# S5 stage: 28 dense tiles beside twelve batches (3, 2, 2) instead of ten, and three gating tiles beside each of the last four

## The reference, cut to what matters

```python
proj = h @ w_in                                  # 1024 -> 2 * 2048
u, z = jnp.split(proj, [D_INNER], axis=-1)
# per group of 16 channels (128 groups), 64 complex states:
lam_bar = jnp.exp(lam * dt)
bu = einsum('blgi,gpi->blgp', u32, b_bar)        # complex
_, states = lax.associative_scan(combine, (a, bu), axis=1)
y = einsum(real(states), c_re) - einsum(imag(states), c_im) + d_skip * u32
y = gelu(y)
y = y * sigmoid(y @ w_glu + b_glu)
y = y * silu(z)
return y @ w_out
```

## Time and profile before

| | us |
|---|---|
| median of 3 runs | 1660.5 (1659.75 to 1662.72) |
| the profiled execution | 1658.89 |
| its span, first to last instruction | 1657.1 |
| TensorE busy | 1611.1 (97%) |
| VectorE busy | 991.1 (60%) |
| ScalarE busy | 725.5 (44%) |
| GpSimd busy | 473.8 (29%) |
| mean granted TensorE clock | 0.997 |

### The profile page before, as it was taken

How to read it: one execution, slowest core, us unless ns; L and a number is a source line. 1 busy time by engine, 2 the same in 40 slices (tenths; PEclk the granted TensorE clock), 3 DMA queues, 4 the chain that set the end, 5 groups by cost and what they waited for, 6 DMA issues and landing times.

```text
span 1657.1 us, 24669 instructions
## 1 busy us (share of the span) xinstructions
PE 1611.1 (97%) x10008; PEld 1283.1 (77%) x10008; DVE 991.1 (60%) x1485; ACT 725.5 (44%) x1128; POOL 473.8 (29%) x169
## 2 busy tenths in 40 slices
PE   9999999999999998999999999998999999999998
PEld 7778688887778876778888886775778888888887
DVE  4356635776999989984573656978874222222123
ACT  4482433334565577665433333336763322222122
POOL 2221124343000000000344432234773344334332
PEclk9999999999999999999999999999999999999999
DMA  5232012334655554546734332322003323332332
GB/s 178 77 102 77 27 52 77 101 102 138 154 144 127 149 148 115 122 125 215 235 117 137 102 100 59 103 63 85 2 8 95 102 78 101 102 85 80 95 88 86
DMA packets 271382, 172.01 MB, mean 104 GB/s; under 512 B 91931, under 2 KB 249974, under 8 KB 271142
## 3 DMA queue, kind: packets, MB, share of 16 engines
q1 hardware_dynamic: 259664, 150.49, 32.8%
q10 hardware_dynamic: 11158, 18.08, 3.2%
q0 software_dynamic: 448, 1.88, 0.3%
HBM read 144.87 MB, written 16.78 MB: 98 GB/s over the span
## 4 chain that ended last, share of the span: by engine, by line
PE 80%; DVE 9%; ACT 4%; SPq 3%; issue 1%; DMA 1%; ACTq 0%; POOL 0%; DVEq 0%; POOLq 0%
PE PS L745 23%; PE PS L746 22%; PE PS L747 22%; SPq L2956 1%; PE PS L1357 1%; PE PA L974 1%; DVE ring_lo L2154 1%; PE PS L1345 1%; SPq L2946 1%; PE PA L998 1%; PE PA L1307 1%; PE PA L1002 1%; PE PA L1097 1%; SPq L2968 1%; PE PA L1099 1%
## 5 line engine op out<-in xcount | busy, mean ns | idle before, releaser
L2891 POOL TENSOR_TENSOR ring_lo<-ring,ring_hi 128x2048 fp32r<-128x2048 f32 (+2 forms) x90 | 394.6, 4385 | 1094.8 <-ACT ring_hi L1507 1092.2
L1507 ACT ACTIVATE ring_hi<-ring 128x2048 fp32r<-128x2048 f32 (+2 forms) x121 | 221.0, 1828 | 205.7 <-PE PS L747 167.6
L746 PE MATMUL PS<-U3l,ring_hi 128*128 128x512 f32 x352 | 139.9, 397 | 0.0
L745 PE MATMUL PS<-U3h,ring_hi 128*128 128x512 f32 x352 | 139.4, 396 | 0.0
L747 PE MATMUL PS<-U3h,ring_lo 128*128 128x512 f32 x352 | 138.9, 395 | 0.0
L2834 DVE TENSOR_TENSOR SF<-PS,rs 128x512 f32<-128x512 f32 x22 | 15.2, 691 | 162.7 <-PE PS L747 162.7
L745 PE MATMUL PS<-HT5h,ring_hi 128*128 128x512 f32 x256 | 105.5, 412 | 0.0
L747 PE MATMUL PS<-HT5h,ring_lo 128*128 128x512 f32 x256 | 101.4, 396 | 0.0
L746 PE MATMUL PS<-HT5l,ring_hi 128*128 128x512 f32 x256 | 101.2, 395 | 0.0
L2055 ACT ACTIVATE SF<-SF 128x512 f32<-128x512 f32 x22 | 13.9, 631 | 170.9 <-DVE SF L2834 170.9
L2154 DVE TENSOR_TENSOR ring_lo<-ring,ring_hi 128x2048 fp32r<-128x2048 f32 x31 | 70.4, 2285 | 18.8 <-ACT ring_hi L1507 18.6
(11 more groups left out here) (501 smaller groups left out, 4057.3 us busy)
## 6 DMA issues: line engine op xcount, KB each, us to landing
ring<-in_gla_w_in SPq DMA_DIRECT2D x20, 1024.0 KB, 5.2
ring<-in_s_w_in SPq DMA_DIRECT2D x16, 1024.0 KB, 6.0
ring<-in_s_w_glu SPq DMA_DIRECT2D x16, 1024.0 KB, 5.7
ring<-in_w_gate SPq DMA_DIRECT2D x22, 512.0 KB, 4.0
ring<-in_w_up SPq DMA_DIRECT2D x22, 512.0 KB, 5.3
ring<-in_w_down SPq DMA_DIRECT2D x16, 704.0 KB, 4.6
ring<-in_w_in SPq DMA_DIRECT2D x9, 1024.0 KB, 5.8
ring<-in_gla_w_out SPq DMA_DIRECT2D x8, 1024.0 KB, 5.7
```

Of the source, the lines that this page charges most:

```text
L745: pe.matmul(dst, w[0], x[0], start=start, stop=False)
L746: pe.matmul(dst, w[0], x[1], start=False, stop=False)
L1507: act.activation(ring_hi[:, n % NSLOT, 0:plan.size[n]], ring[:, n % NSLOT, 0:plan.size[n]], ACT.Copy)\
L2891: pool.tensor_tensor(ring_lo[:, n % NSLOT, at], ring[:, n % NSLOT, at], ring_hi[:, n % NSLOT, at].bitcast(F32), ALU.subtract).then_inc(wlo ...
```

## The change

`BESIDE` is made anew. The 28 dense u and z tiles, in the same order as before, go beside batches 0 to 11 (`Z_DONE` = 11), in the rhythm three, two, two: three beside batches 0, 3, 6 and 9, two beside the other eight. The first twelve gating tiles go beside batches 12 to 15, three each. What was tied to batch GA + 1 = 9 (the last z tile, the high and low parts of the gelu outputs 0 to 7, gelu of 4 to 7, the put-off `by_feature`) is tied to batch 11. `S5_LAST` stays. Since the last gating tile of a batch now uses the loads differently, `LOWS` ends one load earlier than `S5_END`, and a loop behind the batches makes that load's low part. The lists that follow from the tiles (`s5_used`, `LOWS`, SyncE's places) are computed by the same lines as before.

```diff
-BESIDE = [DENSE[3 * b:3 * b + 3] for b in range(GA)] + [DENSE[24:26], DENSE[26:]]
-BESIDE += [[("glu_a", 2 * j), ("glu_a", 2 * j + 1)] for j in range(6)]
+Z_DONE = 11
+BESIDE = [DENSE[(7 * b + 2) // 3:(7 * b + 9) // 3] for b in range(Z_DONE + 1)]
+BESIDE += [[("glu_a", 3 * j + i) for i in range(3)] for j in range(4)]
...
-                if b == GA + 2:
+                if b == Z_DONE + 1:
                     by_feature(b - 1)
 
-                k = KD if b in (GA + 1, NBATCH - 1) else 6
+                k = KD if b in (Z_DONE, NBATCH - 1) else 6
...
-                if b != GA + 1:
+                if b != Z_DONE:
                     by_feature(b)
...
-                if b == GA + 1:
+                if b == Z_DONE:
                     for i in range(4, GA):
                         gelu(i)
...
-                if b == GA + 1:
+                if b == Z_DONE:
 
                     act.wait_ge(gelu_done, GA)
                     act.wait_ge(tile_done, tiles["s5_z"][-1].t + 1)
...
-                if b == GA + 1:
+                if b == Z_DONE:
 
                     scaled(*own_tiles.pop())
                     b_factors(b + 2, first=lambda: fresh_lows(range(4)))
                     fresh_lows(range(4, GA))
                 for n in LOWS[b]:
                     low_weights(n)
-                if b + 2 < NBATCH and b != GA + 1:
+                if b + 2 < NBATCH and b != Z_DONE:
                     b_factors(b + 2)
...
                 for tile in own_tiles[2:]:
                     scaled(*tile)
+            for n in range(LOWS[-1].stop, S5_END):
+                low_weights(n)
             dve.wait_ge(y_ps, NBATCH)
```

## The result

The changed kernel takes 1677.5 us (median of 5 runs, 1674.6 to 1680.0) against 1660.5 before: the ratio is 1.0100, with a 95% interval of 1.0087 to 1.0113. It is 17 us slower. The sign of the forecast was right, its size (+7.1, range up to 1674.5) was not.

A forecast was written before the change was run, and what follows sets the result against it. VectorE was to bound nearly all of batches 0 to 11, TensorE those from 12 on. Batch 15's outputs at 754.5 plus 5.6 for one more tile gave 760.1 against 753.02, +7.1 on 1660.5: 1667.6 us, range 1662.0 to 1674.5.

The forecast's parts named there:

- VectorE's units: VectorE's cost per batch: 15.8 us plus 2.2 for each low-part split (L) and 0.6 for each scaled tile (n).
- Rivals 1 and 2: 1: over sixteen batches idle only moves, 1660 to 1663, chance 0.12; 2: three-tile batches carry VectorE's backlog, about 1652, 0.07.
- SyncE's queue: Loads waiting for the last of three tiles hold outputs at least 23.5 us apart; 0.6 us taken at batch 14.
- The step on three-tile batches: Batches 3, 6 and 9 take VectorE 19.8 us each; its only tile wait is 0.7 us in batch 7.
- the forecast would stay: Clock drops in two-tile batches, up to 1.4 us each, leave TensorE's 231.6 us under VectorE's 245.3 in batches 0 to 11.
- The clock term in front of batch 12: A clock drop after the wait ahead of outputs(12) costs TensorE 1.4 us, from a possible 0 to 1.4.
- Edits at nothing: Split after the loop and last eight high and low parts come some 6 us later, hidden by S5_LAST's tiles: no cost.
- Rival 3: Two-tile batches: VectorE waits for tiles, 0.9 us in each of eight, +7 more, 1674.8 us; chance 0.14.

The follow-up runs named there:

- e6_extra_dve: Changed kernel with glu_a 10 read out ahead of gelu, plus one b_factors operation done twice on VectorE in seven two-tile batches: 1678.3 us.
- e7_rhythm: First half of the change alone: 28 tiles beside twelve batches, but two gating tiles beside each of the last four, eight in S5_LAST: 1669.4 us.
- e2_busy: Changed kernel with twelve idle matmuls ahead of outputs in batches 3, 6 and 9: 1678.3 us.
- e1_tail: Changed kernel, but in batch 15 ScalarE reads out the second gating tile (glu_a 10) ahead of the gelu of 8 to 11: 1671.5 us.
- e8_third_b11: Kernel before, with one third gating tile moved from S5_LAST to batch 11: 1658.0 us.
- e9_third_b10: Kernel before, with one third gating tile moved from S5_LAST to batch 10: 1658.3 us.
- e4_pool_after: Changed kernel with glu_a 10 read out ahead of gelu, and low parts of fifteen loads made by GpSimd, not VectorE: 1724.3 us.
- e3_tail_busy: Changed kernel with both glu_a 10 read out ahead of gelu and idle matmuls ahead of outputs in batches 3, 6 and 9: 1671.6 us.
- e5_pool_before: Kernel before, with low parts of the fifteen loads beside batches 1 to 15 made by GpSimd, not VectorE: 1698.2 us.

## Why the prediction was wrong

- **VectorE's units** (15.8 + 2.2 L + 0.6 n; 19.2, 21.4, 25.1, 18.0 us): right within 0.1 us in every batch in which VectorE waited for no tile. That VectorE becomes the bound beside two tiles was right (e6_extra_dve), and the rhythm costs +9.4 us without the third gating tiles (e7_rhythm). Rivals 1 and 2 fell with it: the two-tile batches stand at 19.2 us, not under 18.5.
- **"SyncE's queue" at batches 4, 10 and 14**: as forecast; outputs(4) came 24.3 us after outputs(3), of which 0.6 is a KM wait, and batch 13 to 14 took 22.8.
- **The step on three-tile batches failed.** I counted 19.8 us each and took the clock for harmless in the first twelve batches ("the forecast would stay"). The drops came at outputs(3), (6) and (9), in front of third tiles that had some 0.5 us of room: VectorE waited 0.9 us for it in each, and in batch 7, where I had 0.7, 1.96. So s(12) was 249.6 us behind s(0), not 246.0: **+3.6**, of which 2.3 go with the clock (e2_busy). I had weighed drops of the clock by TensorE's total (231.6 under 245.3), and a total doesn't see on which side of VectorE's queue the tile lands. Where there was room a drop cost nothing: e6_extra_dve has one at outputs(2), and its batch 2 took 20.43 us like batch 1. Batch 7's wait is mostly not the clock's, since without a drop at outputs(6) it was 1.69 (e2_busy) and 1.51 us (e7_rhythm). TensorE took 23.07 and 22.94 us from outputs(6) to outputs(7) there, where I had 22.1; the kernel before took 22.60 in that place, in the batch in which ScalarE also has the first four gelu outputs, and I hadn't read that row. Where the rest comes from stays open.
- **The clock term in front of batch 12** was put at 1.4 us. The drop lay at 681 to 685 us, ahead of outputs(12) at 689.52, where VectorE was the bound. From o(12) to o(13) it took 22.3 us, not 22.1 + 1.4, and o(12) to o(15) took 67.5 us against 68.6: **-1.1**.
- **"Edits at nothing" was the worst step, and it failed too.** I checked that the late splits and gelu outputs are in time for s5_glu (they were; s5_glu didn't wait), but not the PSUM slot of the tile that is opened behind outputs(15). By parity it is that of gating tile 10, which the change moved from first to second tile of batch 15, and so behind gelu on ScalarE. From o(15) to s5_glu 38.3 us instead of 30.6: **+7.7**, 6.3 of which e1_tail gave back.
- The sum: 7.1 + 3.6 - 1.1 + 7.7 = 17.3 us, the measured growth of the stage. Rival 3 had nearly the time (1674.8) and the sign of the mechanism (VectorE waits for tiles), but laid it into the two-tile batches; it was in three-tile ones and in batch 7, and came to 3.6 us, half of that rival's +7. The rest of the miss is the slot in the tail, which no rival had, so that its time came near was luck.

## What to carry to other kernels

When work is spread over a loop, take the cost of a round on each engine that the round needs, and compare them for each kind of round: an engine at 60% of the span was full in just these rounds, and lighter rounds for TensorE only uncovered it. The place to put a movable tile is a round in which another engine is the bound, which is what e8_third_b11 does, for 2 to 3 us. And when tiles shift their place in a two-slot rotation, write down for each opening of a slot which read-out frees it and what is queued ahead of that read-out; one such entry was worth 6 us here.

## What the runs showed of the hardware

- The clock falls in some executions and not in others at the same place of the program. The changed kernel's trace has 1.2 GHz for 3.4 us at outputs(3), (6) and (9), e1_tail's too, e7_rhythm's only at the third. TensorE had waited 1.9, 2.6 and 2.3 us just before; in e7_rhythm waits of 1.94 and 2.62 us at outputs(3) and (6) left the full clock. Before the change a stretch with a wait of 3.65 us (for WB, at 655 us) kept the full clock; after it a wait for WB of 3.66 us, until 680.8 us, was followed by a drop.
- In the attention stage, some 350 us behind the start of s5_glu, the changed kernel's trace has a granted clock of 0.78 and 0.54 in two stretches of 10 us:

```profile
1140.00:1150.00 10.00, 6.75 (x27) 4.61 (x26) 6.85 (x14) 4.90 (x11) 1.11 (x2) 0.78 0.69 218
1150.00:1160.00 10.00, 9.95 (x50) 6.83 (x49) 5.95 (x29) 5.75 (x20) 3.95 (x7) 0.54 0.34 107
```

  That is 1.2 GHz for some 13.6 us. The traces of e2_busy, e8_third_b11 and e9_third_b10 have the same and that of e4_pool_after nearly; e3_tail_busy, e5_pool_before, e6_extra_dve and e7_rhythm have some 3.4 us of it there, before and e1_tail nothing. From s5_glu to the end of the span it is 882.9 us with the long drop (changed kernel; 883.0 and 883.1 in e8_third_b11 and e9_third_b10, 885.2 in e2_busy with one more drop at 1070 us), 879.3 to 880.3 with the short one, and 879.0 and 878.5 without (before, e1_tail). The edits don't touch this part; some 4 us of one execution can come from there. That it explains runs of one kernel that lie 5 us apart is likely, but not shown, since only one run of each has a trace. What decides whether it happens stays open.
- A GpSimd split (two SBUF inputs, 4.6 to 5.2 us) stops an operation of VectorE with two SBUF inputs until it has ended: 0.70 us became 5.00, and the scan instruction (L2484, TENSOR_TENSOR_SCAN) went from 1.24 to 5.52 in e4_pool_after.
